# Blockwise inverse in 64x64 quarters, two at a time, with the second form read in place and the keys' scores in other banks

## What is computed

```python
a = jnp.where(strict, jnp.einsum('nbhcd,nbhsd->nbhcs', k_beta, k) * decay, 0.0)
t_inv = lax.linalg.triangular_solve(a + eye, eye, left_side=True, lower=True, unit_diagonal=True)
u = jnp.einsum('nbhcs,nbhsd->nbhcd', t_inv, v * beta[..., None])
w = jnp.einsum('nbhcs,nbhsd->nbhcd', t_inv, k_beta * jnp.exp(g)[..., None])
```

## Time and profile before

| | us |
|---|---|
| median of 3 runs | 1432.31 (1432.04 to 1433.28) |
| the profiled execution, its own time | 1431.44 |
| span of the profile | 1429.2 |
| mean granted TensorE clock, share of full | 0.98 |
| PE busy in the span | 1361.6 |
| DVE busy | 780.6 |
| ACT busy | 366.5 |
| POOL busy | 286.5 |

### The profile page before, as it was taken

How to read it: one execution, slowest core, us unless ns; L and a number is a source line. 1 busy time by engine, 2 the same in 40 slices (tenths; PEclk the granted TensorE clock), 3 DMA queues, 4 the chain that set the end, 5 groups by cost and what they waited for, 6 DMA issues and landing times. The chain is left out here.

```text
span 1429.2 us, 20767 instructions
## 1 busy us (share of the span) xinstructions
PE 1361.6 (95%) x7302; PEld 801.2 (56%) x7302; DVE 780.6 (55%) x1593; ACT 366.5 (26%) x797; POOL 286.5 (20%) x529
## 2 busy tenths in 40 slices
PE   8889999999999999999998899989899999899996
PEld 5458576685776857768584433336454544633332
DVE  2856766656666566665556443255435454834227
ACT  3322313223132232332221221203323232222210
POOL 2243316033160340603201200030000000200011
PEclk9989999999999999999998999999999999899998
DMA  6440412405124051240713699970111119199983
GB/s 208 123 106 14 110 51 81 137 13 165 50 68 149 13 165 50 57 154 14 243 63 145 258 413 413 389 264 1 62 38 40 42 40 347 79 357 413 412 323 115
DMA packets 173330, 220.89 MB, mean 155 GB/s; under 512 B 57360, under 2 KB 107920, under 8 KB 173264
## 3 DMA queue, kind: packets, MB, share of 16 engines
q1 hardware_dynamic: 141744, 173.66, 34.9%
q10 hardware_dynamic: 26432, 28.32, 5.8%
q0 software_dynamic: 5088, 18.02, 3.5%
HBM read 185.63 MB, written 34.34 MB: 154 GB/s over the span
## 5 line engine op out<-in xcount | busy, mean ns | idle before, releaser
L509 PE MATMUL bank<-xT,wgu 128*128 128x512 f32 x448 | 196.5, 597 | 3.3 <-DVE wgu L1183 3.3
L1967 PE MATMUL bank<-wgu,moe_xgT 128*32 128x512 f32 x1536 | 169.8, 594 | 1.2 <-issue 0.9
L509 PEld LDWEIGHTS bank<-xT,wgu 128*128 128x128 f32 x448 | 84.5, 191 | 105.2 <-issue 105.2
L557 PE MATMUL bank<-wd,oT 128*128 128x512 f32 x256 | 123.6, 623 | 2.8 <-ACT oT L916 1.6
L591 PE MATMUL bank<-wd,xT 128*128 128x256 f32 x512 | 119.7, 379 | 0.0
L1183 DVE SCALAR_TENSOR_TENSOR wgu<-bank,taps,wgu 128x510 f32<-128x510 f32 (+1 forms) x128 | 95.3, 745 | 41.7 <-ACT wgu L794 36.7
L1967 PEld LDWEIGHTS bank<-wgu,moe_xgT 128*32 128x32 f32 x1536 | 49.1, 110 | 103.6 <-issue 91.8
L591 PEld LDWEIGHTS bank<-wd,xT 128*128 128x128 f32 x512 | 95.3, 190 | 14.4 <-issue 2.9
L1990 PE MATMUL bank<-wd,moe_hidT 128*32 128x512 f32 x768 | 87.0, 593 | 4.1 <-DVE moe_hidT L2238 3.1
L2234 DVE TENSOR_TENSOR moe_hid<-moe_silu,bank 128x256 f32<-128x256 f32 x24 | 10.1, 422 | 126.5 <-ACT moe_silu L2077 126.5
L557 PEld LDWEIGHTS bank<-wd,oT 128*128 128x128 f32 x256 | 47.5, 198 | 52.2 <-issue 49.1
(11 more groups left out here) (352 smaller groups left out, 2319.6 us busy)
## 6 DMA issues: line engine op xcount, KB each, us to landing
wgu<-moe_w_gate SPq DMA_DIRECT2D x32, 1024.0 KB, 13.4
wgu<-moe_w_up SPq DMA_DIRECT2D x32, 1024.0 KB, 14.9
wd<-moe_w_down SPq DMA_DIRECT2D x32, 1024.0 KB, 15.0
wgu<-dn_w_in SPq DMA_DIRECT2D x32, 512.0 KB, 5.2
slots_x<-gains SPq DMA_DIRECT2D x5, 1920.0 KB, 10.9
wd<-dn_w_in SPq DMA_DIRECT2D x8, 1024.0 KB, 6.6
wd<-dn_w_out ACTq DMA_DIRECT2D x16, 512.0 KB, 4.0
xT<-slots_x ACTq DMA_DIRECT2D x16, 512.0 KB, 8.2
```

The costliest lines, as they stand in the source:

```text
L509: mm = pe.matmul(bank[:], wqkv[:, ct, k], xT[:, k], start=k == 0, stop=k == KD - 1)
L557: mm = pe.matmul(ps[uses.at[f"{name}{n}"][0]][:], oT[:, h, tt], wo[:, h, half * 512:(half + 1) * 512], start=h == 0, stop=h == 1)
L1967: mm = pe.matmul(ps[2][seats].rearrange("p (a f) -> p a f", a=2), xgT[:, j % ROW_BUFS, k, seats], wgu[:, e % RING, :, k], start=k == 0, st ...
```

## The change

Three things. At each level `make_x` and `make_v` no longer multiply 128x128 tiles: for each token tile there are two matmuls of 64 rows by 64 columns, `e` = 0 from partitions 0 to 63 and `e` = 1 from partitions 64 to 127. At levels 4 and 5 each writes the half of the bank's partitions that has the same number, at level 6 the other half (`opposite`). The results are packed into 256 columns of the bank. The mask, now 64 columns wide, goes over 256 elements, and at level 6 it is a plain copy, since the quarter has nothing to mask away. `sq` keeps its 128x128 tiles for the transposes; ACT fills the two quarters on the diagonal, each with a copy on 64 partitions, and GpSimd clears `sq` once at the start. `update` is cut into one instruction per half and per block pair: four at level 4, two at level 5 and two at level 6.

Second, `make_v` reads merged U itself; the copy `W` and its semaphore are gone, and `make_v` waits for U's update of the level before. Third, the scores of the next head (`KK`, `KQ`) go to banks 6 and 7 and the transposed values (`tr2`, `tr3`) to 2 and 3. A semaphore `level_open` is raised once by PE ahead of each group; nobody waits for it.

```diff
--- before.py
+++ after.py
...
@@ -60,7 +61,8 @@
     for l in range(BASE, LEVELS):
         b = 1 << l
         at = C_LEV + (l - BASE) * P
-        c[:, at:at + P] = (r // (2 * b) == q // (2 * b)) & (r // b != q // b)
+        one, other = r % HALF, q % HALF
+        c[:, at:at + P] = (one // (2 * b) == other // (2 * b)) & (one // b != other // b)
     i, j = np.arange(4)[:, None], np.arange(4)[None, :]
     c[:, C_JLT:C_JLT + 16] = (j < i).reshape(1, 16)
     c[:, C_BELOW:C_BELOW + 256] = (np.arange(16)[None, :] < np.arange(16)[:, None]).reshape(1, 256)
@@ -115,12 +117,12 @@

 PROJECT = [("proj0", 0), ("proj1", 1), ("proj2", 0), ("proj3", 1)]
-PREPARE = [("tr0", 4), ("tr1", 5), ("tr2", 6), ("tr3", 7)]
+PREPARE = [("tr0", 4), ("tr1", 5), ("tr2", 2), ("tr3", 3)]
 TURN_O = [("oT0", 6), ("oT1", 7)]
 OUTPUT = [(f"y{n}", n % 2) for n in range(8)]
 GATES = [("z0", 0), ("z1", 1)]
 OUTPUT_EARLY, OUTPUT_LATE = [(f"y{n}", 0) for n in range(4)], [(f"y{n}", n % 2) for n in range(4, 8)]
-SCORES = [("KK", 2), ("KQ", 3)]
+SCORES = [("KK", 6), ("KQ", 7)]
 OUTPUT_END = [("y6", 4), ("y7", 5)]

...
...
@@ -305,7 +308,7 @@
             if b < 2:
                 return (y_ready, 1 + (NK - 2) * 8) if uses is LAST else (conv_ready, (i + 1) * 4 + 3 + b)
             if head_zero(i):
-                return {2: (at_ready, 2), 3: (mask_ready, 2), 4: (sq_ready, 2), 5: (keys_ready, 1), 6: (v_ready, 1), 7: (v_ready, 2)}[b]
+                return {2: (v_ready, 1), 3: (v_ready, 2), 4: (sq_ready, 2), 5: (keys_ready, 1), 6: (at_ready, 2), 7: (mask_ready, 2)}[b]
             if b < 4:
                 return vn_ready, (i - 1) * 8 + 6 + b - 1
             if uses is LAST and b < 6:
@@ -324,12 +327,32 @@
             done += (NK - 3) * MAIN.per[b]
             return b, done + k + (NEXT_TO_LAST.per[b] if uses is LAST else 0)

-        def merged(which, h, l, tt=None):
+        def opposite(l, e):
+
+            return 1 - e if l == LEVELS - 1 else e
+
+        def side(e):
+
+            return slice(HALF * e, HALF * (e + 1))
+
+        def diagonal(a, e):
+
+            return a[side(e)].rearrange("p (t n) -> p t n", t=TT)[:, :, side(e)]
+
+        def merged(which, h, l, e, rows, tt=None, part=None):

             b = 1 << l
-            one, other = (TU[which][dd][:, h, 0] for dd in range(2))
+            one, other = (TU[which][dd][side(rows), h, 0] for dd in range(2))
             first, tiles = (0, TT) if tt is None else (tt, 1)
-            return bass.AP(one.tensor, one.offset + first * P, [list(one.ap[0]), [2 * b, tiles * P // (2 * b)], [other.offset - one.offset + b, 2], [1, b]])
+            if l == LEVELS - 1:
+                one = (one, other)[e]
+                runs = [[1, b]]
+            else:
+                runs = [[2 * b, HALF // (2 * b)], [other.offset - one.offset + b, 2], [1, b]]
+            at = one.offset + first * P + HALF * e
+            if part is not None:
+                runs, at = runs[1:], at + 2 * b * part
+            return bass.AP(one.tensor, at, [list(one.ap[0])] + ([[P, TT]] if tt is None else []) + runs)

         def z_pair(a, n):

@@ -616,8 +639,11 @@
                     else:
                         pe.wait_ge(T_ready, i * (2 * NL - 2) + (l - BASE - 1) * 2 + h + 1)
                     bank = begin(uses, f"X{l}{h}", i)
+                    pe.sem_inc(level_open, 1)
                     for tt in range(TT):
-                        mm = pe.matmul(bank[:, tt * P:(tt + 1) * P], A[:, h, tt], merged(0, h, l, tt), start=True, stop=True)
+                        for e in range(2):
+                            to = side(opposite(l, e))
+                            mm = pe.matmul(bank[to, tt * HALF:(tt + 1) * HALF], A[side(e), h, tt, to], merged(0, h, l, e, e, tt), start=True, stop=True)
                     done(mm, uses, f"X{l}{h}")

                 def make_y(l, h):
@@ -629,8 +655,10 @@

                 def make_v(l, h):
                     bank = begin(uses, f"V{l}{h}", i)
+                    pe.sem_inc(level_open, 1)
                     for tt in range(TT):
-                        mm = pe.matmul(bank[:, tt * P:(tt + 1) * P], X[:, h, tt], W[:, h, tt], start=True, stop=True)
+                        for e in range(2):
+                            mm = pe.matmul(bank[side(opposite(l, e)), tt * HALF:(tt + 1) * HALF], X[side(e), h, tt], merged(1, h, l, e, e, tt), start=True, stop=True)
                     done(mm, uses, f"V{l}{h}")

                 for l in range(BASE, LEVELS):
@@ -638,7 +666,8 @@
                     make_x(l, 1)
                     for h in range(2):
                         pe.wait_ge(xm_ready, i * 2 * NL + 2 * (l - BASE) + h + 1)
-                        pe.wait_ge(W_ready, i * 2 * NL + 2 * (l - BASE) + h + 1)
+                        if l > BASE:
+                            pe.wait_ge(U_ready, i * 2 * NL + 2 * (l - BASE) - 2 + h + 1)
                         make_v(l, h)
                     if l < LEVELS - 1:
                         filler()
@@ -862,20 +891,18 @@
                     act.activation(sq[:, n], bank[:], ACT.Tanh, scale=0.5).then_inc(zt_ready, 1)

                 for l in range(BASE, LEVELS):
-                    for h in range(2):
-                        if l > BASE:
-                            act.wait_ge(U_ready, i * 2 * NL + 2 * (l - BASE) - 2 + h + 1)
-                        elif h == 0:
-                            act.wait_ge(T_in, (i + 1) * 16 * P // BLK)
-                        act.copy(W[:, h].rearrange("p t (a e b) -> p (t a) e b", e=2, b=1 << l), merged(1, h, l)).then_inc(W_ready, 1)
                     if uses is FIRST and l == BASE + 1:
                         decays(i + 1)
                     if l < LEVELS - 1:
+                        if uses is FIRST and l == BASE:
+                            act.wait_ge(zeroed, 1)
                         for h in range(2):
                             bank = got(uses, f"V{l}{h}", i)
                             if l > BASE:
                                 act.wait_ge(T_ready, i * (2 * NL - 2) + 2 * (l - BASE) - 2 + h + 1)
-                            act.copy(sq[:, h], bank[:]).then_inc(V_kept, 1)
+                            for e in range(2):
+                                ins = act.copy(diagonal(sq[:, h], e), bank[side(e), 0:TT * HALF].rearrange("p (t n) -> p t n", t=TT))
+                            ins.then_inc(V_kept, 1)
                     if following and l == BASE + 1:
                         act_silu(i + 1, 3)
                 if following:
@@ -963,6 +990,7 @@

         @block.gpsimd
         def _(pool):
+            nc.gpsimd.memset(sq[:], 0.0)
             nc.gpsimd.memset(zeros, 0.0).then_inc(zeroed, 1)

             def prepare(n):
@@ -1304,9 +1332,13 @@

                 def mask_x(l, h):
                     bank = got(uses, f"X{l}{h}", i)
-                    at = C_LEV + (l - BASE) * P
-                    m = c[:, at:at + P].rearrange("p (o a) -> p o a", o=1).to_broadcast([P, TT, P])
-                    nc.vector.tensor_tensor(X[:, h], bank[:].rearrange("p (t n) -> p t n", t=TT), m, ALU.mult).then_inc(xm_ready, 1)
+                    raw = bank[:, 0:TT * HALF].rearrange("p (t n) -> p t n", t=TT)
+                    if l == LEVELS - 1:
+                        nc.vector.tensor_copy(X[:, h], raw).then_inc(xm_ready, 1)
+                    else:
+                        at = C_LEV + (l - BASE) * P
+                        m = c[:, at:at + HALF].rearrange("p (o a) -> p o a", o=1).to_broadcast([P, TT, HALF])
+                        nc.vector.tensor_tensor(X[:, h], raw, m, ALU.mult).then_inc(xm_ready, 1)

                 def update(which, l, h):
                     if which and l < LEVELS - 1:
@@ -1314,8 +1346,18 @@
                         from_v = sq[:, h]
                     else:
                         from_v = got(uses, f"{'YV'[which]}{l}{h}", i)[:]
-                    change = from_v.rearrange("p (a e b) -> p a e b", e=2, b=1 << l)
-                    nc.vector.tensor_tensor(merged(which, h, l), merged(which, h, l), change, ALU.subtract).then_inc(U_ready if which else T_ready, 1)
+                    for e in range(2):
+                        rows = opposite(l, e)
+                        if l == LEVELS - 1:
+                            old, change = merged(which, h, l, e, rows), from_v[side(rows), 0:TT * HALF].rearrange("p (t b) -> p t b", t=TT)
+                            ins = nc.vector.tensor_tensor(old, old, change, ALU.subtract)
+                            continue
+                        parts = HALF >> (l + 1)
+                        change = diagonal(from_v, e).rearrange("p t (a e b) -> p t a e b", a=parts, e=2)
+                        for part in range(parts):
+                            old = merged(which, h, l, e, rows, part=part)
+                            ins = nc.vector.tensor_tensor(old, old, change[:, :, part], ALU.subtract)
+                    ins.then_inc(U_ready if which else T_ready, 1)

                 def z_silu(n):
```

(4 more changed lines are left out.)

## The result

The changed kernel takes 1404.68 us (median of 4 runs, 1403.99 to 1407.3), the kernel before beside it 1432.17 us (4 runs, 1427.01 to 1433.28): a ratio of 0.9824, with 95% interval 0.9804 to 0.9844. The forecast was 1398, so 27.5 us were gained where 34 were expected. The profiled span fell from 1429.2 to 1402.0 us.

A forecast was written before the change was run, and what follows sets the result against it. PE, busy 95% of the span, was taken as the bound; savings of 27.0 us (heads 1 to 6), 4.1 (head 7) and 4.0 (head 0), less 1 for raises, made 34.1 off 1431.44: median 1398, range 1390 to 1408.

The forecast's parts named there:

- A group: X or V products of a level: eight 64x64 matmuls, pairs running together, take 0.46 us instead of 0.92.
- the first rival: X and V groups: pairs run one after another, a group stays at 0.92 us, total 1426 us; chance 16%.
- The division of the array: Each level on PE: going into and out of the divided array costs 0.2 us.
- The scores' wait: End of level 6: PE's wait for the U update ahead of the next head's scores goes, 0.64 us.
- W read in place: Level 4: without ACT's copies, V's wait for W goes, 0.21 us a head.
- Both rivals with slower pairs: X and V groups: pairs one after another, 1426 us, 16%; or each half change empties the array, 1557 us, 6%.
- the third: Rival for X and V groups: pairs together but fed slowly, 0.04 us a record, 0.64 a group, 1406 us; chance 6%.
- What DVE takes back: Levels 4 to 6: longer split updates on DVE delay PE, cutting a head's saving from 5.4 to 4.5 us.
- the forecast wait of 0.5 us at level 5's X: Heads 1 to 6: PE newly waits about 0.5 us for DVE's T update ahead of level 5.
- my working: Length of a level counted from its first X: 2.85 us at level 4, 2.25 at levels 5 and 6.
- A mask's end to V: Levels: V starts 0.06 us after its mask ends.
- the raises: The layer's 96 raises of level_open: 0 to 5.8 us in all, taken as 1 us, mostly standing where PE waits anyway.

The follow-up runs named there:

- halves apart: Changed kernel with the loops of make_x and make_v turned round, all four token tiles of one half before the other's: 1415.95 us, ratio 0.9908.
- the best kernel: Changed kernel with one-instruction updates at levels 4 and 5 and the third early output projection in bank 1: 1395.25 us, ratio 0.9734; repeated, 1392.75 us.

## Why the prediction came out as it did

**What held.** PE set the end, and its work in the levels was halved. A group was put at 0.46 us and is 0.48. The Trainium skill's rule (TensorEngine Tiling, section Restrictions and Gotchas) that row tiles can't use one bank at a time, on which the first rival was built, does not hold for these pairs, which differ in rows and in the partitions they write: 16 of their records take 0.48 us, 30 ns each, where a 128x128 record before took 115. The division of the array was put at 0.2 us a level; from the filler to X at level 5 it is 264.01 - 262.10 = 1.91 us against 1.82 in the old kernel (269.76 less the filler's start at 267.94 in its trace), 0.09 (and not by the raise, as the runs with more raises show), and as the second V group takes 258.51 - 257.90 = 0.61 against 0.48, the way out is 0.13. The scores' wait was put at 0.64 and brought 0.80 by itself; W read in place was put at 0.21 and brought nothing. Both rivals with slower pairs fall; the third's 0.04 us per record is what halves apart would have given.

**What failed** is the step "What DVE takes back". It put DVE's price at 0.9 us a head (5.4 if only PE counts, 4.5 in all). Freed of split updates and of the shared bank, the level stretch is 21.81 - 17.07 = 4.74 us shorter than before, in the changed kernel 2.84: DVE takes back 1.9 us. Two parts of it were measured singly, and the two edits together gave 1.96 us of the period: 1.22 for split updates (0.99 us each instead of the 0.9 I took, and 0.87 instead of 0.65 to 0.8 at level 5), and 0.64 for the third projection, which waits in bank 0 for the sum of the second. This wait was not in my sum at all. I looked for the next late thing at X (DVE's T updates ahead of level 5), not at the fillers between, although the bank table names their bank; the forecast wait of 0.5 us at level 5's X appears as 0.73 one group earlier.

**A smaller term.** PE's own part of the levels is 3.12, 2.38 and 2.38 us in the best kernel against 2.85, 2.25 and 2.25 in my working: 0.5 us a head. A mask's end to V was put at 0.06 us, from the old trace; it is 256.79 - 256.54 = 0.25 at level 4. In the old trace PE was still feeding X when that mask ended, so 0.06 is no price of a wait; where PE waited without a raise it is 0.13, and the raise adds about 0.12. I had called the raises cheap because they stand where PE waits; but they stand behind the wait, so it is just there that they cost. Together: 1.0 (DVE) + 0.5 (PE's part) + 0.13 (rest of the fillers) make the missing 1.66 us of head 2's stretch.

**Heads 0 and 7.** Head 7, counted from its first X to the gate projection (L591, now L614), gave 3.44 us (697.12 to 716.93 became 677.75 to 694.12), 4.1 forecast. Head 0 gave 1.4 of 4.0. Its timeline of PE, beside the earlier trace rows:

```profile
88.54 1.15 PE L646 MATMUL bank<-wgu,wd 64*64 64x64 f32 x32 [3.42 <-DMA wgu<-T_rows]
...
96.39 0.79 PE L646 MATMUL bank<-wgu,wd 64*64 64x64 f32 x16 [2.61 <-DVE wgu L1359]
...
105.74 2.05 PE L600 MATMUL bank<-wgu 128*128 128x128 f32 x16
...
112.72 1.28 PE L712 MATMUL bank<-late,wgu 128*128 128x128 f32 x8 [0.59 <-DVE gains L1258]
```

The levels there lasted 17.20 us instead of 19.72, 2.5 saved where 4.5 were put, since its chain runs through the split updates of levels 4 and 5; with whole ones the period of head 0 is 77.58 us and not 79.48 (79.06 in the second profile). The wait at the first product of the recurrence came (0.59 ahead of it and 0.22 within it, for 0.5).

**The sum.** 1.4 + 16.5 (heads 1 to 6) + 3.4 = 21.4 us where 34.1 were put. The profiled gain is 27.2 because 1.5 us came ahead of head 0's first X and 4.4 behind the layer. Neither was forecast. The start moves as much between two profiles of one kernel (head 0's first X at 88.54 and 89.61 in the changed one). The part behind the layer took 661.3 us before and 656.9 and 659.0 after. There PE runs the same 3869 records in both kernels, and in the first two profiles it is busy with them for 621.73 and 618.28 us at a granted clock of 0.975 and 0.981. So some 3.5 of the 4.4 us go with the clock and are no work that the change saved; 1.7 of them lie in one group, shown at the end, and the idle time ahead of that group is 0.84 shorter. The clock does not explain all that one profile has over another. But the medians gained 27.5 and 26.0 us in two sessions, so 4 to 6 us beyond the heads came each time, and what makes them come stays open.

In the heads, head 7's levels included, the forecast missed 12.7 us, in the profiled span 6.9. That the time fell into the range of 1390 to 1408 was in part luck: with what the heads gave alone it would have been 1431.44 - 21.4 + 0.9 = 1410.9.

## What to carry to other kernels

When the bound engine gets faster, list for the next one every group that waits for it, the fillers and their banks too, not only the group that you made faster. Splitting an instruction by partitions to skip zeros can cost more than computing the zeros: one instruction of 512 elements took 0.69 us, four of 128 took 0.99. To judge an edit to a loop, read the loop's period in one profile (it repeated to 0.02 us here) beside the total, which moved by 3 us and more through code that was not touched, and read the granted clock of a stretch before you explain its length.

## What the runs showed of the hardware

Two 64x64 matmuls in opposite corners of the array, fp32, run at once with one PSUM bank between them, a record each 30 ns if the corners alternate in the queue and each 43 ns if eight of one come first. A semaphore raise by PE between a wait and the matmul behind it costs 0.11 to 0.15 us.

One group far from the change shows what the clock does. The products L1634 of the kernel before (L1676 in the changed one) are code that the change leaves alone. The kernel before, then the changed one:

```profile
945.60 15.67 PE L1634 MATMUL bank<-late 128*128 128x512 f32 x32 [2.04 <-PEq L1817]
```

```profile
921.82 13.97 PE L1676 MATMUL bank<-late 128*128 128x512 f32 x32 [1.20 <-PEq L1859]
```

The same two stretches with the granted clock (length, busy PE, PEld, DVE, ACT, POOL, clock, DMA):

```profile
945.60:961.27 15.67, 15.67 (x34) 6.86 (x35) 12.29 (x17) 0.00 (x0) 5.54 (x6) 0.89 1.00 331
```

```profile
921.82:935.79 13.97, 13.97 (x34) 6.27 (x35) 12.27 (x17) 0.00 (x0) 5.38 (x6) 1.00 0.94 315
```

15.67 x 0.89 is 13.95: the group does the same work, and for part of it the clock stood at the lower of its two levels. In three traces with 128x128 levels it lasts 15.67, 15.67 and 17.04 us, after 2.04, 1.91 and 2.70 us of idle, at a granted clock of 0.89, 0.89 and 0.82. In the ten other traces it lasts 13.97 after 1.20 us of idle, at the full clock. I took this for a trait of the small matmuls until the kernel before with added raises showed 13.97 after 1.20 as well. So the length is the clock's, and in this group the clock was lower only where PE had stood idle longer ahead of it; why PE's sequencer lets it wait 1.20 us in some programs and 1.91 to 2.70 in others was not found.
